# Feed-forward norm sums as high and low products inside the second up tile, without the odd product behind them

## The reference

```python
def rmsnorm(x, g):
    y = x * rsqrt(mean(x * x, axis=-1) + EPS)
    return y * g

def conv_ffn(xn, conv_past, w_up, conv_w, conv_b, w_down):
    h = xn @ w_up                       # 1024 features -> 2 * 2816
    ... causal width-3 convolution over h, then g, u = split(hc)
    return (silu(g) * u) @ w_down
```

## Time and profile before

| what | value |
|---|---|
| time, median of 3 runs | 2081.44 us (2081.0 to 2081.5) |
| time of the profiled execution | 2080.62 us |
| its span, first to last instruction | 2078.7 us |
| PE busy | 2067.0 us, 99% |
| DVE, ACT, POOL busy | 1391.2, 1005.3, 178.8 us |
| PE on the chain that ended last | 98% |

### The profile page before, as it was taken

How to read it: one execution, slowest core, us unless ns; L and a number is a source line. 1 busy time by engine, 2 the same in 40 slices (tenths; PEclk the granted TensorE clock), 3 DMA queues, 4 the chain that set the end, 5 groups by cost and what they waited for, 6 DMA issues and landing times.

```text
span 2078.7 us, 39640 instructions
## 1 busy us (share of the span) xinstructions
PE 2067.0 (99%) x15865; PEld 1965.2 (95%) x15865; DVE 1391.2 (67%) x2638; ACT 1005.3 (48%) x1635; POOL 178.8 (9%) x142
## 2 busy tenths in 40 slices
PE   9999999999999999999999999999999999999998
PEld 8888989998999999999998889889989999999998
DVE  7668786788737763676465787777787477537653
ACT  6267315647527652444352772265565366424433
POOL 0000000000040110011300000000001311001112
PEclk9999999999999999999999999999999999999999
DMA  6231223121222222222232212221212222222222
GB/s 206 79 107 41 92 90 99 52 72 52 62 91 81 81 90 93 81 83 89 92 109 83 95 44 92 89 100 52 72 52 72 74 89 86 86 92 87 85 88 92
DMA packets 54343, 175.20 MB, mean 84 GB/s; under 512 B 7076, under 2 KB 11860, under 8 KB 54212
## 3 DMA queue, kind: packets, MB, share of 16 engines
q1 hardware_dynamic: 47364, 158.88, 24.6%
q0 software_dynamic: 3072, 10.11, 1.2%
q10 hardware_dynamic: 3776, 4.34, 0.6%
HBM read 160.25 MB, written 12.90 MB: 83 GB/s over the span
## 4 chain that ended last, share of the span: by engine, by line
PE 98%; DVE 1%; ACT 0%; DMA 0%; SPq 0%; DVEq 0%; issue 0%
PE d L1523 63%; PE d L1579 15%; PE ab L1626 4%; PE d L1925 2%; PE d L1590 2%; PE d L1934 2%; PE ab L1874 1%; PE ab L1862 1%; PE d L1776 1%; PE d L1630 1%; PE ab L1911 1%; PE ab L1523 1%; PE ab L1681 0%; PE ab L1741 0%; PE d L1733 0%; PE ab L1712 0%
## 5 line engine op out<-in xcount | busy, mean ns | idle before, releaser
L473 ACT ACTIVATE wh<-raw 128x512 fp32r<-128x512 f32 x548 | 345.0, 631 | 716.1 <-PE d L1523 553.7
L845 DVE TENSOR_TENSOR wl<-raw,wh 128x512 fp32r<-128x512 f32 x548 | 378.3, 692 | 281.6 <-ACT wh L473 273.0
L1523 PE MATMUL d<-xh,wh 128*128 128x288 f32 x2400 | 510.7, 293 | 0.9 <-DVE xl L858 0.8
L1523 PE MATMUL d<-xl,wh 128*128 128x288 f32 x2400 | 507.8, 292 | 0.0
L1523 PE MATMUL d<-xh,wl 128*128 128x288 f32 x2400 | 507.8, 292 | 0.0
L1523 PEld LDWEIGHTS d<-xh,wh 128*128 128x128 f32 x2400 | 380.5, 188 | 6.7 <-issue 4.9
L1523 PEld LDWEIGHTS d<-xl,wh 128*128 128x128 f32 x2400 | 380.7, 187 | 0.0
L1523 PEld LDWEIGHTS d<-xh,wl 128*128 128x128 f32 x2400 | 380.7, 187 | 0.0
L1579 PE MATMUL d<-xh,wh 128*128 128x288 f32 x768 | 173.6, 307 | 0.0
L1579 PE MATMUL d<-xh,wl 128*128 128x288 f32 x768 | 164.5, 295 | 0.0
L1579 PE MATMUL d<-xl,wh 128*128 128x288 f32 x768 | 164.1, 295 | 0.0
(11 more groups left out here) (325 smaller groups left out, 3220.4 us busy)
## 6 DMA issues: line engine op xcount, KB each, us to landing
raw<-in_w SPq DMA_DIRECT2D x286, 512.0 KB, 3.5
out_o_k<-k POOLq DMA_DIRECT2D x4, 1152.0 KB, 7.0
out_o_v<-v POOLq DMA_DIRECT2D x4, 1024.0 KB, 8.8
x<-in_xT SPq DMA_DIRECT2D x8, 288.0 KB, 5.1
k<-in_bc_k_past ACTq DMA_DIRECT2D x4, 512.0 KB, 4.3
v<-in_bc_v_past ACTq DMA_DIRECT2D x4, 512.0 KB, 5.4
out_y<-z SPq DMA_DIRECT2D x4, 432.0 KB, 2.7
raw<-in_w SPq DMA_DIRECT2D x4, 256.0 KB, 5.6
```

What stands on the lines that cost most here:

```text
L473: act.activation(wh[:, c % SPLIT_SLOTS, :], stored, ACT.Copy).then_inc(high_done, 1)
L845: dve.tensor_tensor(lows, stored, highs, ALU.subtract).then_inc(low_done, 1)
L1523: ins = pe.matmul(outs[half], w_, r_[:, kk, HALF * half:HALF * half + HALF], start=first and n == 0 and begin, stop=last and n == len(kks) ...
```

## The change

The two sums of the feed-forward norm are no longer taken between the first and the second up tile in plain float32. ACT rounds `sumsq` to a high part `sumh` (semaphore `sum_high`), DVE subtracts it to a low part `suml` (`sum_low`). PE multiplies both with `none`, a float32r matrix of minus ones that the kernel holds already, in four matmuls of 288 columns, behind the second feature block (`kk == 1`) of the second up tile. ACT's logarithm gets the scale with a minus sign to make up for it. The odd product behind the second tile goes. The sums of the other norms stay as they are.

```diff
+            [("before_suml", [P, 2944], F32), ("suml", [P, T], F32R), ("before_sumh", [P, 3 * T], F32), ("sumh", [P, T], F32R)])
...
-            def rsqrt_of(count, part=slice(0, T)):
+            def rsqrt_of(count, part=slice(0, T), sign=1.0):
...
-                act.activation(rstd[:, part], norm_both[:, part], ACT.Ln, bias=eps[:], scale=1.0 / D_MODEL).then_inc(lns, 1)
+                act.activation(rstd[:, part], norm_both[:, part], ACT.Ln, bias=eps[:], scale=sign / D_MODEL).then_inc(lns, 1)
...
                     ffn_high(f, 0, 0)
                     if f == 0:
-                        rsqrt_of(2 * l + 2)
+                        act.wait_ge(last_sum, l + 1)
+                        act.activation(sumh[:], sumsq[:], ACT.Copy).then_inc(sum_high, 1)
+                        rsqrt_of(2 * l + 2, sign=-1.0)
...
                 low_parts(l, 2 * U_OUT + 2 * KD + 3)
+                dve.wait_ge(last_sum, l + 1)
+                dve.wait_ge(sum_high, l + 1)
+                dve.tensor_tensor(suml[:], sumsq[:], sumh[:].bitcast(F32), ALU.subtract).then_inc(sum_low, 1)
...
+            def split_sum(l):
+
+                pe.wait_ge(sum_high, l + 1)
+                pe.wait_ge(sum_low, l + 1)
+                for part, first, last in ((sumh, True, False), (suml, False, True)):
+                    for half in range(2):
+                        ins = pe.matmul(norm_out[half], none, part[:, HALF * half:HALF * half + HALF], start=first, stop=last)
+                ins.then_inc(norms, 1)
...
+                def second_sum(kk):
+                    if kk == 1:
+                        split_sum(l)
...
                         up(f, 0, 0, xn_wait(l, 2))
-                        norm_sum(2 + 2 * l)
-                        up(f, 0, 1)
-                        pe.wait_ge(dfree[0], START + l * (D_USES // 2) + 1 + D_UP // 2)
-                        odd_product(l * CHUNKS + 4, 0, 2 * U_UP, xh)
+                        up(f, 0, 1, behind=second_sum)
```

More of the change, by code:

```diff
@@ L177, in encoder @@
             [("hi", [P, 1920], F32R), ("lo", [P, 1920], F32R), ("sample_q", [P, PAIRS, 2 * TS], F32)])
-        w1, w2, r1l, _, iq, sq, sumsq, hb, cv, at, _, hx, _, xp = shared(
+        w1, w2, r1l, _, iq, sq, sumsq, hb, cv, at, _, hx, _, xp, _, suml, _, sumh = shared(
             [("w1", [P, 2944], F32), ("w2", [P, 2944], F32)],
@@ L183, in encoder @@
             [("before_hx", [P, 2944 + 1920], F32), ("hx", [P, 1024], F32R)],
-            [("before_xp", [P, 2944 + 2 * T], F32), ("xp", [P, KD, 2 * TS], F32R)])
+            [("before_xp", [P, 2944 + 2 * T], F32), ("xp", [P, KD, 2 * TS], F32R)],
+            [("before_suml", [P, 2944], F32), ("suml", [P, T], F32R), ("before_sumh", [P, 3 * T], F32), ("sumh", [P, T], F32R)])
         scores = sb("scores", [P, 1152])
@@ L243, in encoder @@
         first_squares, last_square, last_sum = sem("first_squares"), sem("last_square"), sem("last_sum")
+        sum_high, sum_low = sem("sum_high"), sem("sum_low")
         first_half, last_x, samples_paired = sem("first_half"), sem("last_x"), sem("samples_paired")
@@ L1533, in norm_sum @@
             def norm_sum(count):
[L1535 to L1538, removed]
+                pe.wait_ge(acc_ready, count)
                 sum_half(0, sumsq)
                 sum_half(1, sumsq).then_inc(norms, 1)
+            def split_sum(l):
[5 more added lines that the diff above has]
+                ins.then_inc(norms, 1)
             def xn_wait(l, r):
@@ L2020, in _, with up @@
                     project(l, U_OUT + j, D_OUT + j, xn_wait(l, 1) if j == 0 else no_wait)
-                def up(f, i, s, wait=no_wait):
+                def second_sum(kk):
+                    if kk == 1:
+                        split_sum(l)
+                def up(f, i, s, wait=no_wait, behind=no_wait):
                     pe.wait_ge(dfree[s], START + l * (D_USES // 2) + f * (D_HALF // 2) + i + D_UP // 2)
-                    dense(l * CHUNKS + f * (2 * U_HALF) + 4 * i, wait, 2 * U_UP + 2 * s, dhalf[s], xh, xl, range(KD))
+                    dense(l * CHUNKS + f * (2 * U_HALF) + 4 * i, wait, 2 * U_UP + 2 * s, dhalf[s], xh, xl, range(KD), behind=behind)
                 for f in range(2):
```

## The result

The changed kernel takes 2100.47 us, median of four runs (2099.77 to 2100.94), against 2081.47 (2081.0 to 2082.15) before: a ratio of 1.0093, 95% interval 1.0082 to 1.0105. It is 19.0 us slower. The forecast was 2080.0; one of its rivals, the slow rhythm coming in at the new products in both layers and staying, was priced at 2100.5.

What follows compares the result with a forecast made beforehand. PE was taken as the bound, its time being matmul count times spacing. From 2080.62 us, minus 1.43 for two layers plus 0.04 for the wait, came 2079.2 profiled; the median, 0.82 above, was forecast at 2080.0, range 2078.8 to 2091.5.

Steps and rivals of the forecast that it cites:

- What bounds the kernel: PE, busy 99% of the span; feed-forward time is the number of matmuls times their spacing, with no wait to remove.
- The seam: Last pair of first up tile to second pair of loop: 28 pairs in 7.28 us against 8.00, 0.72 gained a layer.
- ACT and DVE: Added work beside PE: low part ready about 0.02 us late, root 1.1 us later, at no cost to the loop.
- The fast rhythm kept in both layers: Likeliest case: the new products leave matmuls 0.1299 us apart through both feed-forward parts; chance 0.62, of which 0.58 the forecast.
- the late load: First low-part weight load at the new products, taken as 0.02 us late, costing 0.04 us for both layers.
- The first rival: Slow rhythm enters at the new products and stays: 10.5 and 9.9 us, both layers 2100.5; chance 0.17, one layer 0.18.
- other weights: Rival's condition at the new products: weights unlike the stream's might, as the float32 sums did, turn the rhythm slow.
- another bank: Rival's condition at the new products: writing a different bank in mid-tile might, as the float32 sums did, turn the rhythm slow.
- The point from which it decides is any start of that matmul that is later than 0.13 us behind its predecessor: Rival's threshold at the first new matmul that waits: a start later than this would let the slow rhythm in.
- The reasons against the rival: Earlier streams: no rhythm change by a wait, only by other forms; `ab` writes and eight `xl` waits leave it fast.
- What restores it is the odd product: 128-column product before the loop: ends the slow rhythm; removing it was sized as a gain of 0.12 us a layer.

Runs made afterwards that it cites:

- e12: Changed kernel with the new products behind the third feature block and the minus ones moved by 480 bytes to a multiple of 256; 2079.72 us, ratio 0.9995.
- e1: Changed kernel with the four new products behind the third feature block instead of the second; 2100.34 us, ratio 1.0092.
- e13: Changed kernel, products still behind the second feature block, with the minus ones moved by 480 bytes to a multiple of 256; 2100.48 us, ratio 1.0077.
- e6: Kernel before plus four unread products on `xh` in a down tile, weights the running `wh` block (first layer) or minus ones (second); 2088.72 us, ratio 1.0036.
- e4: Changed kernel with the waits kept behind the second feature block, the products moved behind the fourth; 2091.06, 2101.25 and 2090.81 us, ratio 1.0064.
- e11: Kernel before plus four unread products, weights the minus ones moved by 32 bytes (first layer) or `wh` shifted by 32 bytes (second); 2095.42 us, ratio 1.0069.
- e14: Kernel before plus four unread products, weights the `wh` block shifted by 256 bytes (first layer) or 128 bytes (second); 2088.49 us, one run.
- e15: Kernel before plus four unread products, weights the `wh` block shifted by 64 bytes (first layer) or not shifted (second); 2088.85 us, one run.
- e5: Changed kernel with the new products behind the third feature block and the odd product kept; 2080.04 us, ratio 0.9995.
- e3: Changed kernel with the odd product kept in front of the loop; runs of 2100.04, 2090.32, 2100.31 and 2101.07 us, ratio 1.0077.
- e8: Kernel before without its two odd products in the feed-forward part, float32 sums kept; 2101.63 us, ratio 1.0099.

## Why the prediction was wrong, point by point

- **What bounds the kernel**: right. PE's spacing is the time; no engine and no transfer came between.
- **The seam**: the sum of 7.28 us for 28 pairs was right, e12 has 7.28. The change has 7.41, since the 0.13 "if the new products leave the rhythm fast" weren't had.
- **ACT and DVE**: right. The subtraction ends 1.58 us behind the last addition, as forecast. The load is 16 and 24 ns late, where I took 20. ACT's logarithm comes 2.55 us behind the last pair of the first tile, 1.43 before: 1.12 later, forecast 1.1, and no wait arose from it.
- **The fast rhythm kept in both layers (0.62)**: this step failed. The sum takes the new products to leave the fast rhythm as it is, and enters the late load with 0.04 us. The runs showed two things in its place, each enough to turn the rhythm: four weight loads that start 32 bytes above a multiple of 256 (e1), and one load that comes some 20 ns late (e13). In the changed kernel, which has both, the stretches behind the second tiles take 10.55 and 10.01 us longer.
- **The first rival**: its price was right, 10.5 and 9.9 forecast (its terms add up to 2100.6 rather than 2100.5). That is no luck, since the spacing was read from rows of the same stream. Its condition was right in part: the late low part and the "other weights" are in it; "another bank" is not a cause (e6). It had a chance of 0.17, and the range left it out.
- **"The point from which it decides is any start of that matmul that is later than 0.13 us behind its predecessor"**: wrong. In the first layer the matmul started 0.127 behind, and the rhythm turned. What counts is the load: its time (e4, e13) or its start (e1, e11, e14, e15).
- **The reasons against the rival**: "that stream shows no change of rhythm by a wait" was read from a stream that was slow before and behind the wait; it could say nothing of a fast one. e4 shows a wait that turns it. The eight waits for `xl` in the first tile made no load late (the loads start 129 to 131 ns apart throughout), so they could say nothing either. And "only by other forms" overlooked that two loads of one form can differ in where they start.
- **"What restores it is the odd product"**: too strong. It does so in before and e5, and in e3 it doesn't. I sized it as a cost of 0.12; by e8 its removal from the kernel before costs 20 us. In the changed kernel its absence is not the cause: with it kept (e3) three runs of four are as slow.

The prediction weighed the Trainium skill, TensorE: Matmul & The Clock Gate, section LDWEIGHTS: by its 0.107 us a load 0.02 late still ends in time. The profile shows each load as 0.19 us long, but the trace agrees as to the one matmul: it starts 0.110 and 0.105 us behind the start of its late load, where 0.130 is the rule, and moved by 3 ns at most. It also shows that this isn't all a late load does. The Trainium skill, on the same page, section Back-to-back issue gap, gives one sustained spacing for a stream's column count, and none for 288; here one form at a granted clock of 1.00 has two, 0.130 and 0.133, and which of them holds decides 20 us.

## What to carry to other kernels

Where a stream of matmuls bounds a kernel, divide the length of long stretches by their counts, and look for more than one value at one clock; then find the instruction at which it changes. A product put into such a stream should have its weights start where the others do (here, at a multiple of 256 bytes) and its operands ready well before its load is due, as e12 does. A saving of 1 us is not worth a place where the operands come just in time.

## What the runs showed of the hardware that I had not expected

- The same matmuls (288 columns, float32r, granted clock 1.00) run in two rhythms that hold themselves for 400 us: starts alternate 128 and 132 ns, or 129 and 131 (mean 130), or repeat 131, 131, 132, 140 (mean 133.3).
- Four weight loads in a row that start 32, 64 or 128 bytes above a multiple of 256, or a single one that comes some 20 to 30 ns late (150 to 161 ns behind the load before it in e4 and e13), turn the fast one into the slow one, with no idle time of PE at that place. Both were shown each without the other. How late a load may come before it does this was not tried.
- Why there are two rhythms stays open. So does whether the start has to be a multiple of 256 or only to agree with the loads around it: weights all of which start elsewhere weren't tried. For the float32 sums the form was not told apart from the start of the ones. The odd product's weights are a block of `wh`, so its effect doesn't come from where they start.
- The best version is e12, 1.1 us under before by the medians, with an interval that includes no change.
